# Handing expert gathers on in pairs instead of fours in a two-layer hybrid encoder with a product-key expert layer

## What is computed

```
q = (yt @ w_q).reshape(T, PEER_HEADS, 2, PEER_HALF)        # 8 heads
s = jnp.einsum('thpc,pnc->thpn', q, sub_keys)
val, idx = lax.top_k(s, PEER_TOPK)                         # 16 of 128, twice
cand = val[:, :, 0, :, None] + val[:, :, 1, None, :]
top_val, top_pos = lax.top_k(cand.reshape(...), PEER_TOPK) # 16 of 256
gate = softmax(top_val)
ub = jnp.take(u, eb, axis=0)                               # 16 experts a head and token
act = gb * gelu(jnp.einsum('thkd,td->thk', ub, xb))
vb = jnp.take(v, eb, axis=0)
out = jnp.einsum('thk,thkd->td', act, vb)
```

## Time and profile before

| what | value |
|---|---|
| median of 3 runs | 1606.82 us (1606.29 to 1609.34) |
| the profiled execution, its own time | 1606.77 us |
| its span, first to last instruction | 1605.0 us |
| mean granted TensorE clock | 0.767 of full speed |
| busy: PE, DVE, ACT, POOL | 65%, 69%, 29%, 31% |
| moved by DMA | 646.70 MB, 403 GB/s on average |

### The profile page before, as it was taken

One profiled execution on the slowest core, in us unless ns is written; L12 is line 12 of the kernel. 1 busy time (PEld: TensorE's weight loads), 2 busy tenths in 40 slices (PEclk: granted clock), 3 DMA queues, 4 the chain that ended last, 5 costly groups with the idle time before them and its releaser, 6 DMA issues.

```text
span 1605.0 us, 19986 instructions
## 1 busy us (share of the span) xinstructions
PE 1046.8 (65%) x6936; PEld 711.0 (44%) x6936; DVE 1111.9 (69%) x3119; ACT 461.3 (29%) x953; POOL 500.8 (31%) x541
## 2 busy tenths in 40 slices
PE   8997876757734577778574477877576444544454
PEld 8995642525511266656362155665263111211111
DVE  3436878676457776997756777987765777777764
ACT  4111553111111345742111335743222111111110
POOL 0003333333223333332322323332332333333330
PEclk9998877867955699888796589877788555555666
DMA  9979999999999999999999999999999999999994
GB/s 369 408 259 402 374 420 421 417 421 420 416 420 420 421 378 415 420 415 394 422 416 420 421 411 403 417 405 374 420 418 419 421 422 421 421 421 423 420 420 190
DMA packets 105300, 646.70 MB, mean 403 GB/s; under 512 B 11632, under 2 KB 15728, under 8 KB 37616
## 3 DMA queue, kind: packets, MB, share of 16 engines
q0 software_dynamic: 76032, 553.68, 83.5%
q1 hardware_dynamic: 25536, 89.66, 14.2%
q10 hardware_dynamic: 3632, 2.08, 0.4%
HBM read 644.33 MB, written 1.05 MB: 402 GB/s over the span
## 4 chain that ended last, share of the span: by engine, by line
DMA 40%; PE 28%; DVE 15%; POOL 5%; issue 5%; ACT 4%; DVEq 2%; POOLq 0%; ACTq 0%
DMA ring<-in_uv_dram,expert 36%; PE ps L691 14%; DVE ring L1221 7%; PE ps L868 7%; POOL ring L406 5%; DMA wring<-in_wall_dram 5%; PE ps L881 2%; DVE side L1276 2%; PE ps L698 1%; PE ps L909 1%; ACT side L590 1%; PE ps L856 1%; ACT yg L471 1%; ACT osb L651 1%; ACT L475 0%
## 5 line engine op out<-in xcount | busy, mean ns | idle before, releaser
L1221 DVE CUSTOM_DVE_ANT_0 ring<-ring,ps 128x1024 f32<-128x1024 f32 x528 | 634.8, 1217 | 314.9 <-DMA ring<-in_uv_dram,expert 261.2
L406 POOL DMA_INDIRECT ring<-in_uv_dram,expert x528 | 498.7, 945 | 1068.8 <-PE ps L868 808.2
L868 PE MATMUL ps<-ring,mix 128*32 128x512 f32 x2112 | 369.3, 834 | 327.3 <-DVE mix L1237 327.3
L868 PEld LDWEIGHTS ps<-ring,mix 128*32 128x32 f32 x2112 | 67.8, 135 | 531.7 <-DVE mix L1237 391.0
L665 ACT ACTIVATE gel<-dots 128x4 f32<-128x4 f32 x132 | 27.1, 205 | 761.7 <-DVE dots L1221 761.4
L691 PE MATMUL ps<-yT,wring 128*128 128x128 f32 (+1 forms) x1184 | 159.6, 294 | 48.2 <-DMA wring<-in_wall_dram 27.6
L691 PEld LDWEIGHTS ps<-yT,wring 128*128 128x128 f32 x1184 | 150.7, 202 | 63.6 <-DMA wring<-in_wall_dram 34.2
L881 PE MATMUL ps<-sel,osb 128*128 128x16 f32 x528 | 84.1, 304 | 70.6 <-ACT osb L651 70.6
L881 PEld LDWEIGHTS ps<-sel,osb 128*128 128x128 f32 x528 | 80.7, 241 | 108.9 <-ACT osb L651 108.9
L590 ACT ACTIVATE side<-ident,params 128x128 f32<-128x128 f32 x310 | 96.3, 389 | 15.6 <-PE ps L909 14.8
L856 PE MATMUL ps<-ident,yg 128*128 128x128 f32 x264 | 48.0, 342 | 58.0 <-DVE dots L1221 58.0
(11 more groups left out here) (211 smaller groups left out, 1135.5 us busy)
## 6 DMA issues: line engine op xcount, KB each, us to landing
wring<-in_wall_dram SPq DMA_DIRECT2D x102, 512.0 KB, 11.8
ring<-in_wall_dram SPq DMA_DIRECT2D x44, 512.0 KB, 14.5
kept<-in_wall_dram SPq DMA_DIRECT2D x24, 512.0 KB, 17.0
ring<-in_uv_dram,expert POOLq DMA_INDIRECT x528, 16.1
out_dram<-fo ACTq DMA_DIRECT2D x16, 64.0 KB, 6.7
hT<-in_xT_dram ACTq DMA_DIRECT2D x1, 576.0 KB, 15.9
hT<-in_xT_dram SPq DMA_DIRECT2D x2, 256.0 KB, 3.2
params<-in_smalls_dram ACTq DMA_DIRECT2D x1, 380.0 KB, 17.7
```

The source lines that it names most:

```text
L406: pool.indirect_dma_start(out=ring[:, i % R, :], out_offset=None, in_=uv, in_offset=bass.IndirectOffsetOnAxis(ap=expert[:, n % 2, k:k + 1] ...
L868: mm = pe.matmul(po[32 * j:32 * j + 32, half, :], mix[:, k, :], ring[:, slot, D + 512 * half:D + 512 * (half + 1)], start=(q == 0), stop=( ...
L1221: nc.vector.tensor_tensor_reduce(out=row, in0=row, in1=yrep, scale=1.0, scalar=0.0, op0=ALU.mult, op1=ALU.add, accum_out=dots[:, k:k + 1]) ...
```

## The change

The chain from Gelu to the freed slot is done for pairs of gathers (e = 0 to 7) instead of quarters. `values` and `weights` take e, and their semaphores count eight steps a group. On ACT both Gelus of a quarter stand before its `front` and `side`. On DVE the first pair's `weights` stands behind the second dot and its piece of `side`, the second pair's where the quarter's stood, behind the piece of the route. On PE pair 2q stands where the quarter stood, and pair 2q + 1 behind it; in quarter 3 pair 6 now comes ahead of the next group's `rows`, and pair 7 behind it. Amounts of arithmetic and of data are the same.

```
@@ ACT
                 for q in range(4):
-                    act.wait_ge(s_dot, TOPK * n + 4 * q + 4)
-                    act.activation(gel[:, 4 * q:4 * q + 4], dots[:, 4 * q:4 * q + 4], ACT.Gelu).then_inc(s_gel, 1)
+                    for e in (2 * q, 2 * q + 1):
+                        act.wait_ge(s_dot, TOPK * n + 2 * e + 2)
+                        act.activation(gel[:, 2 * e:2 * e + 2], dots[:, 2 * e:2 * e + 2], ACT.Gelu).then_inc(s_gel, 1)
                     front(4 * n + q)
                     side(n, q)
@@ PE
-            def values(n, q):
-                pe.wait_ge(s_m, 4 * n + q + 1)
-                if q == 0 and n:
+            def values(n, e):
+                q = e // 2
+                pe.wait_ge(s_m, 8 * n + e + 1)
+                if e == 0 and n:
                     pe.wait_ge(s_oe, n)
                 for half in range(2):
-                    for j in range(4):
+                    for j in (2 * (e % 2), 2 * (e % 2) + 1):
                         k = 4 * q + j
...
                 if n:
-                    values(n - 1, 3)
+                    values(n - 1, 7)
                     back(n - 1)
                 for q in range(4):
                     front(4 * n + q)
                     side(n, q)
+                    values(n, 2 * q)
                     if q < 3:
-                        values(n, q)
+                        values(n, 2 * q + 1)
@@ DVE
-            def weights(n, q):
-                ks = slice(4 * q, 4 * q + 4)
-                if q == 0:
+            def weights(n, e):
+                ks = slice(2 * e, 2 * e + 2)
+                if e == 0:
...
-                dve.wait_ge(s_gel, 4 * n + q + 1)
+                dve.wait_ge(s_gel, 8 * n + e + 1)
...
                         elif n:
                             side(n - 1, 3, i)
+                        if i == 1:
+                            weights(n, 2 * q)
...
-                    weights(n, q)
+                    weights(n, 2 * q + 1)
```

More of the change, by code:

```diff
@@ L956, in _ @@
                         final_sums(n - 1)
-            values(N - 1, 3)
+            values(N - 1, 7)
             back(N - 1)
@@ L1234, in weights @@
                 if n:
-                    dve.wait_ge(s_vm, TOPK * (n - 1) + 4 * q + 4)
+                    dve.wait_ge(s_vm, TOPK * (n - 1) + 2 * e + 2)
                 dve.drain()
-                nc.vector.tensor_tensor(mix[:, ks, 0:GT], coef[:, ks].unsqueeze(2).to_broadcast([P, 4, GT]),
-                                        sel[:, :].unsqueeze(1).to_broadcast([P, 4, GT]), ALU.mult).then_inc(s_m, 1)
+                nc.vector.tensor_tensor(mix[:, ks, 0:GT], coef[:, ks].unsqueeze(2).to_broadcast([P, 2, GT]),
+                                        sel[:, :].unsqueeze(1).to_broadcast([P, 2, GT]), ALU.mult).then_inc(s_m, 1)
             def add_back(n):
```

## The result

The changed kernel takes 1680.52 us (median of 4 runs, 1679.68 to 1681.63) against 1606.74 us for the kernel before, measured beside it (1606.29 to 1609.34). The ratio is 1.0454, with a 95% interval of 1.0439 to 1.0470: 4.5% slower. The forecast was 1648 us and the range 1616 to 1668. The direction held, but the time lies above the range, and the loss is 1.8 times the one predicted: 74 us instead of 41.

The account below looks back on a forecast made before the run. The kernel was taken as bound by gathers at the DMA's full rate, except where too few are in flight. Block 2's 22, the first block's 15 and layer 0's 4 us added to 1606.8 gave about 1648 us; range 1616 to 1668.

Parts of the forecast that it names:

- Layer 0: Stretch from 216 to 283: extras of six quarters, two waits and two pairs 6 cost 4 us (bounds 0 and 10).
- PE, 5.8 us a block: Ahead of the long convolution stretch: a pair costs PE a quarter's 1.92 us, three times on the path.
- DVE's own work, 0.55 us a quarter: Every quarter: a second coefficient and mix take 0.55 us more, 73 us for 132 quarters, nothing in the quiet stretch.
- The first Gelu of group 20, 6.4 us: Start of group 20: DVE asks after two dots and stands still 6.4 us for ACT's Gelu (bounds 0 and 7).
- Block 2, 22 us: Groups 18 to 21: 22/0 is issued 24 us late with a cover of 1.7, costing 22 us.
- The waits of group 21: Group 21: waits for the first Gelu and for pair 2's Gelu, 6 us for both (bounds 3 and 10).
- Block 1, 15 us: Groups 11 to 14: same build gives 21, but more gathers in flight at its start, so 15 us (bounds 5 and 21).
- The end, 0 to -1.7: End of the kernel: the last pair takes the last quarter's 3.64 us, so 0, down to -1.7 with the clock up.
- Rival A: Waits for Gelu partly absorbed by gather waits or ACT catching up: half of each stretch's term, 1627 us; chance 0.27.
- Rival B: Slots come free sooner, so DMA restarts sooner where few gathers are in flight: 1597 us; chance 0.07.
- Rival C: No difference: cover takes up all delays, as in the quiet stretch, 1607 us; chance 0.06.
- Rival D: PE becomes the bound from 640 to 700: 3 us a block, in the range, not the sum; no separate chance.

Follow-up runs that it names:

- the wait alone: Changed kernel with both pairs' coefficients, mixes and products at the quarter's old places, plus DVE's early wait for Gelu (quarter 0: also exponentials): 1.0375.
- late pairs: Changed kernel with both pairs' coefficients and mixes at the quarter's end and both pairs of products at the old places: 1.0054, 1617.34 us.
- without the wait: Changed kernel with both pairs of products at the old places and first pairs' coefficients made of constants, so DVE waits for neither Gelu nor exponentials: 1.0052.
- behind the dots: Changed kernel with the first pair's coefficients and mix behind the quarter's fourth dot, and pair 6 behind the next group's rows: 1.0124.

## Where the prediction was right, and why its size was wrong

**The step that failed is the sum of the waits, "22 + 15 + 4 = 41 on 1606.8"**: the mechanism named there (DVE asks after two dots for a Gelu that ACT does not have) is the cause, shown by the pair of runs with the wait alone and without it. But two of the three terms were mis-sized. Layer 0, put at 4 us, measured 17, and the first block, put at 15, measured 27; together they are 25 of the 33 us that are missing. Too few waits were counted, and for layer 0 at the wrong place.

A count of DVE's waits in the changed kernel against the one with late pairs shows the rule. It takes waits of more than 0.15 us, and a group runs from its first dot to that of the next. The ten groups are 0, 1, 10 to 13 and 18 to 21:

```
                        ten groups          other 23 groups
us of waits for       late   changed        late   changed
Gelu                   7.0     68.7          0.0     89.3
exponentials           1.3     11.3          0.0      0.0
the next rows         13.4     32.8         29.9     41.2
gathers                5.5      2.0        226.8    127.4
all else              35.0     11.7         15.2     13.6
sum                   62.1    126.5        271.9    271.5
```

The ten groups are together 64 us longer in the changed kernel, and their waits grew by 64; DVE is busy 377 us in them in both kernels. The other 23 groups hold 89 us of waits for Gelu and are in sum not longer (0.3 us): their waits for gathers shrank by 99. So the new waits cost about their length where DVE had few gathers to wait for, and nothing where it had many. The rows come later too, by 19 us in the ten groups; with pair 6 behind the rows (1.0397) that is 11.

- **PE, 5.8 us a block: wrong.** A pair alone costs what was said (1.91 us), but two pairs behind each other take 1.94 together, and the whole edit of PE's loop leaves the time at 1.0001. The rule of the Trainium skill that the prediction weighed (TensorEngine Tiling (Array Packing), Tiling Modes, Key Properties: different tiles work in parallel) holds here for strips of two pairs too: 1.94 us for both. What PE's order costs is pair 6 ahead of the rows, 0.006 or some 9 us in the whole kernel. At the place where the prediction put it, it does not show: from the first dot of group 17 to that of group 19 the changed kernel loses 7.8 us, and the one with pair 6 behind the rows 9.0.
- **DVE's own work, 0.55 us a quarter: about right.** With ACT's share it is 0.0054, 9 us, where the forecast's terms for the three stretches hold some 12.
- **The first Gelu of group 20, 6.4 us: right**, 3.04 + 3.19 = 6.2 us. Half of it is for the exponentials, which the prediction did not name. At the starts of groups 21, 12 and 13 the two waits together are 6.5, 4.6 and 4.9 us.
- **Block 2, 22 us: 26** (first dot of group 24 less that of group 17, over before; 71.7 - 45.8). The waits of group 21, put at 6 us with bounds of 3 and 10, are 3.3 + 3.2 + 3.6 = 10.1. The wait of 5.5 us in quarter 3 of group 18 was not foreseen; the PE term of 5.8 us, which stood at about that place, was not there. That this term came out so near is in part luck: one error stood in for the other.
- **Block 1, 15 us: 27** (first dot of group 16 less that of group 9, over before; 44.6 - 17.4). The discount from 21 to 15 for more gathers in flight had no row behind it, and quarter 3 of group 10 (7.5 us) was missed in the same way.
- **Layer 0, 4 us: 17.** I costed only the stretch from 216 to 283. The loss is made in groups 0 and 1 (121 to 216), which the prediction never looked at: DVE waits 15.3 us for the first Gelu of the program, of which 6.7 were there before, and some 8 us in group 1 for Gelus and exponentials.
- **The end, 0 to -1.7: right**, the last rows of the table go from 75.2 to 74.6, and the change there alone gives 1.0001.
- **Rival A** (partly absorbed) named a true process: 89 us of waits for Gelu were absorbed. It was wrong that the stretches at issue would absorb half. **Rival B** (slots free sooner) is refuted even without the wait. **Rival C**, no difference, is refuted by the result. **Rival D**, PE as the bound, does not appear: without the wait PE's products are busy for 475 us instead of 369, and the time is that of the late pairs.

Of the signs named beforehand: DVE's waits for Gelu are 158 us, not some 40; slices below 400 stand around both norms, and in layer 0 (slices 4 to 7) as well; the quiet stretch is at 420. The range was too narrow: its upper bounds of 10 us for layer 0 and 21 for the first block were both passed. (The bounds that the prediction lists add up to 1631 and 1664 us, not to 1632 and 1668; the measured time lies outside either.)

What stays open: why the rows still come 11 us later in the ten groups with pair 6 behind them, and why 0.007 is left behind the dots. Neither was traced.

## What to carry to other kernels

Before an instruction is moved ahead in one engine's program, look up what the engine that feeds it has queued ahead of the value, at every place where the code repeats: the wait is set by that queue (copies, table loads, projections that wait for weights), not by the 0.2 us of the operation itself. Price such a wait only where the waiting engine has no slack to give, group by group over the whole span; where it waited for data anyway, 89 us of new waits cost nothing here. And ask what the early result is for: here the slots of quarter 1 came free two dots sooner and found no list of experts to fill them with.

## What the runs showed of the hardware that was not expected

Four products on two column strips (eight records) take 1.91 us at the full granted clock. Eight on all four strips (sixteen records) take 1.92 when they are issued round by round over four strips, and 1.94 as two pairs one behind the other. So the busy time of these products is 571.0 us in the changed kernel and 369.3 before, with no more work, and 371.8 where the pairs always stand together: of packed products, busy time tells how they were fed, not how much PE had to do.
